# RWKV decays at the chunks' ends: 16 products of four columns, in one run or one by one behind the steps of the value projection

## The reference, cut to what matters

```
xr, xw, xk, xv, xa, xg = [h + xx * mu[i] for i in range(6)]     # xx = shifted h minus h
r, k, v = xr @ w_r, xk @ w_k, xv @ w_v
w = -softplus(-(w0 + tanh(xw @ w1) @ w2)) - 0.5
a = sigmoid(a0 + (xa @ a1) @ a2)
g = sigmoid(xg @ g1) @ g2
decay = exp(-exp(w))
state = state * decay_t + (state @ a_t) b_t + v_t k_t           # token by token, 16 heads of 64
```

## Time and profile before

| what | us |
|---|---|
| median of 3 runs | 1269.24 (1268.19 to 1270.05) |
| the profiled execution | 1270.04 |
| its span | 1268.2 |
| TensorE busy in it | 1155.5 (91%) |
| VectorE busy | 736.2 (58%) |
| ScalarE busy | 281.7 (22%) |

### The profile page before, as it was taken

How to read it: one execution, slowest core, us unless ns; L and a number is a source line. 1 busy time by engine, 2 the same in 40 slices (tenths; PEclk the granted TensorE clock), 3 DMA queues, 4 the chain that set the end, 5 groups by cost and what they waited for, 6 DMA issues and landing times.

```text
span 1268.2 us, 19866 instructions
## 1 busy us (share of the span) xinstructions
PE 1155.5 (91%) x8447; PEld 854.9 (67%) x8447; DVE 736.2 (58%) x1189; ACT 281.7 (22%) x475; POOL 92.7 (7%) x86
## 2 busy tenths in 40 slices
PE   6999999899876668999999999899998889999997
PEld 5865647776433333897578888667868874788886
DVE  5546553533221112765588877677874567887774
ACT  5412332331000001534100000325344321000000
POOL 2011000010000000120000000000110532000000
PEclk9999999889888888999999999999899999999999
DMA  9653126169999999532965551334300318655600
GB/s 345 221 198 133 67 83 252 63 246 388 420 421 419 421 421 402 191 143 68 317 207 178 177 186 67 100 124 158 108 2 4 129 47 279 227 177 178 197 1 34
DMA packets 106495, 247.20 MB, mean 195 GB/s; under 512 B 7121, under 2 KB 61408, under 8 KB 93986
## 3 DMA queue, kind: packets, MB, share of 16 engines
q1 hardware_dynamic: 106212, 245.71, 53.1%
q0 software_dynamic: 144, 0.15, 0.0%
q10 hardware_dynamic: 46, 0.01, 0.0%
HBM read 244.80 MB, written 1.05 MB: 194 GB/s over the span
## 4 chain that ended last, share of the span: by engine, by line
PE 81%; DMA 8%; DVE 5%; SPq 2%; ACT 2%; issue 1%; POOL 0%; DVEq 0%
PE bank L486 15%; PE bank L488 15%; PE bank L487 15%; DMA arena<-expert_w_gate 8%; PE bank L351 7%; PE bank L337 4%; PE bank L1399 4%; PE bank L1414 2%; PE bank L2521 2%; SPq L307 1%; PE bank L2502 1%; PE bank L2393 1%; PE bank L470 1%; PE bank L1450 1%; PE bank L1104 1%
## 5 line engine op out<-in xcount | busy, mean ns | idle before, releaser
L486 PE MATMUL bank<-work_rounded,work_rounded 128*128 128x512 f32 (+2 forms) x768 | 301.6, 393 | 11.4 <-DVE work_rounded L1775 5.2
L488 PE MATMUL bank<-work_rounded,work_rounded 128*128 128x512 f32 (+2 forms) x768 | 296.1, 385 | 0.0
L487 PE MATMUL bank<-ring_w_rounded,work_rounded 128*128 128x512 f32 (+2 forms) x640 | 246.8, 386 | 0.0
L486 PEld LDWEIGHTS bank<-work_rounded,work_rounded 128*128 128x128 f32 x768 | 144.2, 188 | 40.2 <-issue 7.8
L488 PEld LDWEIGHTS bank<-work_rounded,work_rounded 128*128 128x128 f32 x768 | 144.2, 188 | 27.1
L487 PEld LDWEIGHTS bank<-ring_w_rounded,work_rounded 128*128 128x128 f32 x640 | 120.8, 189 | 21.0 <-issue 0.5
L1399 PE MATMUL bank<-arena 128*32 128x256 f32 x896 | 72.4, 445 | 45.5 <-DMA arena<-expert_w_gate 39.4
L1293 ACT ACTIVATE arena<-bank 128x256 f32<-128x256 f32 x52 | 20.0, 384 | 414.0 <-PE bank L488 336.5
L1775 DVE TENSOR_TENSOR ring_w_rounded<-arena,work_rounded 128x1024 fp32r<-128x1024 f32 x84 | 102.9, 1225 | 2.9
L1774 DVE CAST work_rounded<-arena 128x1024 fp32r<-128x1024 f32 (+1 forms) x140 | 93.8, 670 | 0.3
L1399 PEld LDWEIGHTS bank<-arena 128*32 128x32 f32 x896 | 37.9, 127 | 75.8 <-issue 64.7
(11 more groups left out here) (421 smaller groups left out, 1637.8 us busy)
## 6 DMA issues: line engine op xcount, KB each, us to landing
arena<-expert_w_up SPq DMA_DIRECT2D x29, 1024.0 KB, 22.3
arena<-expert_w_down SPq DMA_DIRECT2D x28, 1024.0 KB, 26.4
arena<-expert_w_gate SPq DMA_DIRECT2D x27, 1024.0 KB, 16.8
arena<-ffn_w_gate SPq DMA_DIRECT2D x22, 1024.0 KB, 5.5
arena<-ffn_w_up SPq DMA_DIRECT2D x22, 1024.0 KB, 8.1
arena<-ffn_w_down SPq DMA_DIRECT2D x22, 1024.0 KB, 5.2
arena<-hy_w_in SPq DMA_DIRECT2D x12, 856.0 KB, 12.5
arena<-w_in SPq DMA_DIRECT2D x8, 1024.0 KB, 13.7
```

Source lines behind the costliest of these rows:

```text
L486: nc.tensor.matmul(out, lhsT[0], rhs[0], start=first, stop=False)
L487: nc.tensor.matmul(out, lhsT[0], rhs[1], start=False, stop=False)
L488: return nc.tensor.matmul(out, lhsT[1], rhs[0], start=False, stop=last)
```

## The change

The loop over the 16 products between `cumulative(0)` and the value projection goes. The bank for `fraw` is still taken at that place. `key_linear` gets an argument `beside`, a function that it calls in its first column half: after the three matmuls of each step `k` of token tile `t`, it issues the product of tile `t` and piece `q = k`, behind the last step after the signal of the projection's own output. The signal of `fraw` goes with the product of tile 1 and piece 7. The programs of the other engines are the same.

```
-        def key_linear(pe, name, rings, x_ready, second=None):
+        def key_linear(pe, name, rings, x_ready, second=None, beside=None):
...
                     mm = three_passes(ps[:, :], (x_high[name][:, k, tok], x_low[name][:, k, tok]),
                                       (w_high(name, c, k0)[:, k - k0], low[:, k - k0]), k == 0, k == KD - 1)
+                    if beside is not None and c == 0 and k < KD - 1:
+                        beside(t, k)
                 mm.then_inc(full[rings[t]], 1)
+                if beside is not None and c == 0:
+                    beside(t, KD - 1)
...
             cumulative(0)
-            ps = fill(pe, "D", "fraw")
-            for t in range(T):
-                for q in range(NP_):
-                    o = (q * T + t) * 4
-                    sq_ = s_[:, t, q * P:(q + 1) * P]
-                    mm = nc.tensor.matmul(ps[:, o:o + 4], sq_, C("rwends"), start=True, stop=True)
-            mm.then_inc(full["D"], 1)
-            key_linear(pe, "w_rv", "AA", lambda t, half: pe.wait_ge(sem("x_low"), COUNT_FROM["f"] + 6))
+            ends = fill(pe, "D", "fraw")
+
+            def chunk_ends(t, q):
+                o = (q * T + t) * 4
+                mm = nc.tensor.matmul(ends[:, o:o + 4], s_[:, t, q * P:(q + 1) * P], C("rwends"), start=True, stop=True)
+                if t == T - 1 and q == NP_ - 1:
+                    mm.then_inc(full["D"], 1)
+            key_linear(pe, "w_rv", "AA", lambda t, half: pe.wait_ge(sem("x_low"), COUNT_FROM["f"] + 6), beside=chunk_ends)
             cumulative(1)
```

## The result

The changed kernel takes 1277.42 us in the median of four runs (1276.79 to 1279.21), the kernel before 1269.64 on the same occasions (1268.19 to 1270.93). The ratio is 1.0082 with a 95% interval of 1.0053 to 1.0111: slower, by an interval that lies clear of no change. The forecast was 1277.5 us.

A forecast was written before the change was run, and what follows sets the result against it. TensorE, busy 91% of the span, was taken to bound the kernel. The gate's first product 5.9 us late plus 2.4 of half clock gave 8.3: 1278.3 us profiled, 1277.5 on the median; range 1273.0 to 1280.5.

The forecast's parts named there:

- The pause in front: Before the value projection TensorE waits for ScalarE to free a bank, until 893.2; of 4.46 us only 1.4 are gained.
- The products between the steps: In the value projection's first half, two weight loads stay bare per product: 0.224 us each, 3.6 us for 16.
- A: Rival for the value projection's first half: the products' loads hide behind wide matmuls, 3.6 us go, 1273.9 us; chance 0.13.
- C: Rival for the value projection's first half: each product drains the array, 0.5 us each, 4.5 us more, 1282.0; chance 0.06.
- The clock behind the pause: In the value projection's first half, half clock from 892.6 to 896.0 loses 1.4 us; bounds 0 and 3.1.
- VectorE, ScalarE, TensorE: Late result holds VectorE's copy, its key work, ScalarE's exponentials, then the gate's first product: 5.9 us late, TensorE idle 4.8.
- The clock in the gate: In the gate's first product, half clock after TensorE's second pause loses 2.4 us; bounds 0 and 3.5.
- To the end: Behind 945 us nothing covers the delay, TensorE being busy 187 of the last stage's 192 us; the shift goes through.
- rival D: Rival for the later stages: the chain is late but a later stage makes it good, 1269 to 1271 us; chance 0.04.
- B: Rival: late result harmless, only TensorE's own queue counts, the gate's product starts 3.9 us early, 1265.3 us; chance 0.03.

The follow-up runs named there:

- the run with eight: Changed kernel reordered: eight products and one wide float32 product in the bank wait, the other eight in pairs behind the projection's first four steps; ratio 0.9998.

## Why the prediction was right

Its steps, in distances from the first cumulative product, so that the 1.9 us of head start drop out (the forecast's 886.75 is zero).

**The pause in front.** Forecast 893.2, a distance of 6.4; measured 6.4, and 6.2 to 6.3 in five other runs whose pause or filling ended in the same wait (6.6 in the run with eight). Of the old run only 1.5 us were gained.

**The products between the steps.** Forecast 0.224 us each; measured 0.91 - 0.68 = 0.23 in one step at full clock, 0.24 over all 16. Rivals A (the loads hide) and C (0.5 us each) are out. The size fits two bare loads of 0.112 us; which of the three loads they are is argued and not shown. The Trainium skill says ("TensorE: Matmul & The Clock Gate", "Step-by-step: what each phase is for") that the next tile's weights load while this tile's matmul runs. The trace agrees for the wide matmuls (0.227 us apart, with loads of 0.19); for four-column ones it shows 0.112 us from one to the next, with nothing wide to hide the load.

**The clock behind the pause.** The term was mis-sized. The forecast was 2.8 us of work at half clock, 1.4 lost; it was half for 6.3 us, 3.1 lost, the upper bound that was kept (2.9 by the run with wide work in the pause). The copy so came at 24.1 us instead of the 22.5 that 909.2 means.

**VectorE, ScalarE, TensorE.** 17.7 us from copy to the end of the key work were forecast, and 925.50 + 1.22 - 908.98 = 17.74 measured; 1.08 for the two exponentials, 1.08 measured; a pause before the gate of 4.8, 4.59 measured. The first link is what the run with the copy behind the key work takes away, and what the two runs with one late product make out of nothing.

**The clock in the gate.** Forecast 2.4; gate 1 to gate 2 went from 8.0 to 9.8, 1.8 lost.

**To the end.** Forecast was that nothing behind takes it back, and nothing did: rival D is out, and B with it, since the slack that it needs is not there.

By the second gate product the sum is 7.7 + 1.8 = 9.5 against 8.3 forecast: 1.7 more for the first half clock, 0.6 less for the second. The times moved by 0.82% of 1269.64, 10.4 us (6.7 to 14.1), by the ratio, or by 7.8 between the medians; the hit to a tenth of a microsecond is luck, the mechanism and the size are not.

## What to carry to other kernels

Before work is moved behind other work on one engine, ask when its last result is read and what stands behind the reader: a result with one signal is as late as its last piece, and an engine that goes through its program in order stands with all of its later work, as VectorE did for 9.60 us. A run of small instructions that looks like cost on the path can be the cover of a wait; the run with one product, which leaves the work out, prices the gain before any schedule is tried, here about 0.2%. And a cost found in the new kernel is a loss only so far as the old kernel did not have it: of 2.9 us of half clock in the first half, 2.3 were there before.

## What was not expected of the hardware

The fall of the clock behind the front pause had a date. In the six profiled executions that had it, the clock fell 5.8 to 6.1 us after the first cumulative product, though that product lay anywhere from 881.1 to 886.8 us into the span. The date is older than the stretch: in all ten executions the product comes 403.5 to 404.0 us after the clock's last rise, which ends the half clock among the experts at 477.5 to 483.0 us of the span, so the two move together. Four-column work, an empty pause or the one product that stays all stood in front of such a fall. In the run with eight, where one wide float32 product of 0.9 us lies in the middle of eight four-column ones, the clock stayed at 1.00; this is one execution. Where the clock fell, the time that it stayed at half differed: 3.4 us in the run with one product, 6.8 in the others; why is not settled.
